# Seven-product (Strassen) form for 28 gate weight tiles ahead of the attention stage of a decoder layer

## What is computed

```python
mod = silu(c) @ w_ada + b_ada; shift, scale, gate = split(mod, 3)
h = rmsnorm(x, norm_w) * (1 + scale) + shift
aq, ak, av, az, mq, mk, mv, mo, mz, mi, mf, ga, gm = split(h @ w_in)
att = sliding_window_attention(rope(aq), rope(ak), av, sinks)       # 16 heads, 4 kv heads, window 128
y_att = (att * silu(az)) @ w_att
mq = silu(causal_conv(mq)); mk = silu(causal_conv(mk)) * 256 ** -0.5 # width 4
hm = mlstm(mq, mk, mv, mi, mf)                                       # 4 heads of 256
hm = rmsnorm(hm) * m_norm_w * sigmoid(mo)
y_m = (hm * silu(mz)) @ w_m
merged = sigmoid(ga) * y_att + sigmoid(gm) * y_m
out = rmsnorm(x + gate * (merged @ w_out), final_norm_w)
```

## Time and profile before

| | |
|---|---|
| median of 3 runs | 1346.77 us (1346.77, 1346.91, 1345.74) |
| span of the profiled execution | 1343.5 us |
| TensorE busy | 97% of the span |
| TensorE weight loads | 83% |
| VectorE | 48% |
| ScalarE | 32% |
| GpSimd | 45% |
| DMA over the span | 67 GB/s of mean |

### The profile page before, as it was taken

One profiled execution on the slowest core, in us unless ns is written; L12 is line 12 of the kernel. 1 busy time (PEld: TensorE's weight loads), 2 busy tenths in 40 slices (PEclk: granted clock), 3 DMA queues, 4 the chain that ended last, 5 costly groups with the idle time before them and its releaser, 6 DMA issues.

```text
span 1343.5 us, 20127 instructions
## 1 busy us (share of the span) xinstructions
PE 1308.8 (97%) x6941; PEld 1112.3 (83%) x6941; DVE 644.1 (48%) x1343; ACT 427.4 (32%) x1065; POOL 609.3 (45%) x824
## 2 busy tenths in 40 slices
PE   4899999999999999999999999999999999999997
PEld 3687988889788888889888988898889888788886
DVE  5776775857750000354554355435544421544335
ACT  5556564554630000133313332323232211311111
POOL 3507052160634444592665176517660555567240
PEclk9899999999999999999999999999999999999999
DMA  9702011020211310420410041004100133331602
GB/s 327 194 17 64 17 48 33 1 63 0 56 49 54 94 48 30 126 64 1 110 47 16 0 109 47 16 0 119 53 16 16 47 110 94 110 94 47 204 26 100
DMA packets 124951, 89.44 MB, mean 67 GB/s; under 512 B 12370, under 2 KB 117986, under 8 KB 124899
## 3 DMA queue, kind: packets, MB, share of 16 engines
q1 hardware_dynamic: 121056, 76.09, 20.2%
q10 hardware_dynamic: 3842, 12.68, 2.8%
HBM read 80.36 MB, written 8.41 MB: 66 GB/s over the span
## 4 chain that ended last, share of the span: by engine, by line
PE 92%; DVE 4%; ACT 2%; issue 1%; DMA 1%; ACTq 0%; POOL 0%; DVEq 0%
PE pp L574 27%; PE pp L575 26%; PE pp L576 26%; PE pp L742 2%; PE pp L853 2%; PE pp L725 1%; PE pp L726 1%; PE pp L733 1%; PE pp L662 1%; PE pp L845 1%; PE pp L710 1%; DVE prob_t L1485 1%; PE pp L648 1%; DMA freq<-inv_freq 1%; DVE pp L1423 1%
## 5 line engine op out<-in xcount | busy, mean ns | idle before, releaser
L513 POOL TENSOR_TENSOR w_hi<-raw,ones 128x256 fp32r<-128x256 f32 x388 | 263.9, 710 | 614.0 <-ACTq L371 342.3
L574 PE MATMUL pp<-h_hi,w_hi 128*128 128x512 f32 x896 | 349.9, 391 | 0.1
L575 PE MATMUL pp<-h_lo,w_hi 128*128 128x512 f32 x896 | 349.0, 390 | 0.0
L576 PE MATMUL pp<-h_hi,w_lo 128*128 128x512 f32 x896 | 348.8, 389 | 0.0
L517 POOL TENSOR_TENSOR w_lo<-raw,w_hi 128x256 fp32r<-128x256 f32 x388 | 319.7, 854 | 7.6
L576 PEld LDWEIGHTS pp<-h_hi,w_lo 128*128 128x128 f32 x896 | 168.2, 188 | 35.3
L574 PEld LDWEIGHTS pp<-h_hi,w_hi 128*128 128x128 f32 x896 | 168.3, 188 | 34.7 <-issue 0.7
L575 PEld LDWEIGHTS pp<-h_lo,w_hi 128*128 128x128 f32 x896 | 168.3, 188 | 33.5
L574 PE MATMUL pp<-w_hi,h_hi 128*128 128x256 f32 (+2 forms) x496 | 154.8, 312 | 2.0 <-ACT v_tok L1049 1.2
L576 PE MATMUL pp<-w_hi,h_lo 128*128 128x256 f32 (+2 forms) x496 | 153.1, 309 | 0.0
L575 PE MATMUL pp<-w_lo,h_hi 128*128 128x256 f32 (+2 forms) x496 | 152.9, 308 | 0.0
(11 more groups left out here) (259 smaller groups left out, 1928.1 us busy)
## 6 DMA issues: line engine op xcount, KB each, us to landing
raw<-w_in SPq DMA_DIRECT2D x70, 512.0 KB, 3.9
w_mod<-w_ada SPq DMA_DIRECT2D x6, 1024.0 KB, 12.7
x_in<-x SPq DMA_DIRECT2D x4, 1024.0 KB, 10.0
raw<-w_att SPq DMA_DIRECT2D x8, 512.0 KB, 5.6
merged_dram<-mix_a ACTq DMA_DIRECT2D x8, 512.0 KB, 2.6
w_gate<-w_ada ACTq DMA_DIRECT2D x8, 512.0 KB, 3.6
raw<-w_m SPq DMA_DIRECT2D x8, 512.0 KB, 3.8
mix_in<-merged_dram ACTq DMA_DIRECT2D x8, 512.0 KB, 3.3
```

The source lines that it names most:

```text
L513: ins = pool.tensor_tensor(hi[:, q, :], raw[:, s, q, :], one[:, q, :], ALU.mult)
L574: pe.matmul(o, lh, rh, start=first, stop=False)
L575: pe.matmul(o, lh, rl, start=False, stop=False)
L576: return pe.matmul(o, ll, rh, start=False, stop=last)
```

## The change

28 of the 32 tiles that only feed a sigmoid or a silu leave their stages: ga 2 to 7, gm 0 to 5, mz 0 to 7 and mo 0 to 7. They are computed in a new stage between the start and A, two tiles at a time, as 14 pairs (`GATE_PAIRS`: ga, gm and then mz with mo of the same number).

**Products.** For a pair the two weight tiles A and B and h are seen as 2 x 2 blocks (features in by two tiles; features in by two token halves), and the four blocks of the result come from 7 products by Strassen's scheme (Winograd's form) in place of 8. One product is 4 slices x 3 passes = 12 matmuls of 128x512 (`product`), into one of 8 banks; a later product of the same pair may accumulate onto a bank of an earlier one. The operand of a product is a block of weights or one of four differences and sums of blocks, `sums` and in place in `raw` (DVE `sum_of`, for the first two pairs partly GpSimd `first_sum`); ACT makes its high half (`operand_high`), GpSimd its low half (`operand_low`), in a ring of ten (`RING`). On the other side four combinations of h's quadrants are needed once, `t_hi` and `t_lo` (DVE `token_sum`, `token_low`; ACT `token_high`). DVE adds the products' banks into blocks (`add_first`, `add_seventh`, `block_22`, `block_21`, `block_12`), ACT applies sigmoid or silu (`gate_out`), and for mz with mo DVE multiplies the two and the norm weight (`gate_products`). SP stores the results to `sig_dram` and `gate_dram` and loads them again in B (`load_sig`), C (`gate_m`, one load a head) and D2 (`sig_m`).

**Start.** The loads of the first two pairs (four tiles of 512 KB) stand in SP's queue ahead of `load_mod(2)` and `load_mod(3)`. Product 0 stands ahead of the last `turn_mod`. `first_two_units` is gone: all eight token units of the first head are separate ones. The products of the first two pairs are interleaved.

**The stages that lost tiles.** B has 10 tiles (`B_TILES`). C has 16 units a head: mq, mk, mv, with the last chunk of a head behind mq 0 of the next and its transpositions behind mq 3; the mLSTM loop is unrolled, and its slots are 2, 3, 4, 2 for mq and mk and 0, 1 for mv. D1 has two tiles, gm 6 and 7, in slots 0 and 1, and holds the end of the last head between its units. `D_SLOTS` is now 2, 4, 0, 1. The gate sum is made in D2, one step behind each of eight units. E is as it was.

```diff
-SLOT_USES = {"A": (4,) * 5, "B": (4, 4, 4, 4, 0), "C": (8,) * 5,
-             "D1": (2, 2, 2, 0, 2), "D2": (2, 2, 2, 0, 2), "E": (1, 1, 1, 1, 0), "E2": (1, 1, 1, 1, 0)}
-SLOT_DMAS = {"A": (4, 3, 8, 4, 4), "B": (4, 4, 4, 4, 0), "C": (8,) * 5,
-             "D1": (2, 2, 2, 0, 2), "D2": (2, 2, 2, 0, 2), "E": (1, 1, 1, 1, 0), "E2": (1, 1, 1, 1, 0)}
-D_SLOTS = (0, 1, 2, 4)
+SLOT_USES = {"A": (4,) * 5, "B": (3, 3, 2, 2, 0), "C": (4, 4, 8, 4, 4),
+             "D1": (1, 1, 0, 0, 0), "D2": (2, 2, 2, 0, 2), "E": (1, 1, 1, 1, 0), "E2": (1, 1, 1, 1, 0)}
+SLOT_DMAS = {"A": (4, 3, 8, 4, 4), "B": (3, 3, 2, 2, 0), "C": (4, 4, 8, 4, 4),
+             "D1": (1, 1, 0, 0, 0), "D2": (2, 2, 2, 0, 2), "E": (1, 1, 1, 1, 0), "E2": (1, 1, 1, 1, 0)}
+D1_SLOTS = (0, 1)
+D_SLOTS = (2, 4, 0, 1)
 FIRST = 4
-BANK_USES = {"A": 24, "B": 16, "C": 48, "D1": 8, "D2": 8, "E": 8}
+GATE_SUM_AT = 3
+BANK_USES = {"A": 24, "B": 10, "C": 32, "D1": 2, "D2": 8, "E": 8}
 
...
-C_UNITS = [("mq", 0), ("mq", 1), ("mq", 2), ("mq", 3), ("mk", 0), ("mk", 1), ("mk", 2), ("mk", 3)]
-for _u in range(NB):
-    if _u % 2 == 0:
-        C_UNITS.append(("mz", _u // 2))
-    C_UNITS.append(("mv", _u))
-C_UNITS += [("mo", 0), ("mo", 1), ("mo", 2), ("mo", 3)]
-
-C_LOADS = [(MQ, 0, 0), (MQ + P, 1, 0), (MK, 2, 0), (MK + P, 3, 0), (MZ, 4, 0),
-           (MVC, 0, 1), (MVC + P, 1, 1), (MZ + P, 2, 1), (MO, 3, 1), (MO + P, 4, 1)]
+C_UNITS = [("mq", n) for n in range(4)] + [("mk", n) for n in range(4)] + [("mv", n) for n in range(NB)]
+
+C_LOADS = [(MQ, 2, 0), (MQ + P, 3, 0), (MK, 4, 0), (MVC, 0, 0), (MVC + P, 1, 0), (MK + P, 2, 1)]
+C_PER = {0: 1, 1: 1, 2: 2, 3: 1, 4: 1}
+
+B_TILES = [("ga", 0, 0, 0), ("wa", 0, 1, 0), ("ga", 1, 2, 0), ("wa", 1, 3, 0), ("wa", 2, 0, 1), ("wa", 3, 1, 1),
+           ("wa", 4, 2, 1), ("wa", 5, 3, 1), ("wa", 6, 0, 2), ("wa", 7, 1, 2)]
...
-C_SLOT = {"mq0": (0, 0), "mq1": (1, 0), "mk0": (2, 0), "mk1": (3, 0), "mz0": (4, 0), "mz1": (2, 1),
-          "mo0": (3, 1), "mo1": (4, 1)}
-C_MASK_AFTER = 2
+C_SLOT = {"mq0": (2, 0), "mq1": (3, 0), "mk0": (4, 0), "mk1": (2, 1)}
...
+GATE_PAIRS = [("a", 2), ("a", 4), ("a", 6), ("m", 0), ("m", 2), ("m", 4)] + [("o", t) for t in range(KT)]
...
+PRODUCTS = (1, 6, 7, 5, 2, 4, 3)
+EARLY = [(p, prod) for prod in (1, 5, 2, 3, 7, 6, 4) for p in range(2)]
+G_ORDER = EARLY + [(p, prod) for p in range(2, NG) for prod in PRODUCTS]
+G_AT = {pair_product: g for g, pair_product in enumerate(G_ORDER)}
+RING = 10
+FIRST_OPS = 4
+RING_OFF = (RING - 1 - (len(G_ORDER) - 1)) % RING
...
+TOKENS = {1: ("h", 0, 0), 2: ("h", 1, 0), 3: ("h", 1, 1), 4: ("t", 1, 0), 5: ("t", 0, 0), 6: ("t", 1, 1), 7: ("t", 0, 1)}
...
             load_mod(1)
+            for k in range(2):
+                for p in range(2):
+                    load_pair_slot(p, k)
             load_mod(2)
             load_mod(3)
...
+            def product(g):
+                p, prod = G_ORDER[g]
+                q, slot = p % 2, (g + RING_OFF) % RING
+                kind, kh, th = TOKENS[prod]
+                hi, lo = (h_hi, h_lo) if kind == "h" else (t_hi, t_lo)
+                o = bank({1: 0, 2: 0, 6: 2, 3: 4, 5: 4, 4: 6, 7: 6}[prod] + q)
...
+                t = slice(th * HALF, (th + 1) * HALF)
+                for k in range(HK):
+                    kt = kh * HK + k
+                    if p == 0 and kind == "h":
+                        pe.wait_ge(h_lo_ready, kt + 1)
+                    pe.matmul(o, op_hi[:, slot, k, :], hi[:, kt, t], start=first and k == 0, stop=False, skip_group_check=True)
+                    pe.matmul(o, op_hi[:, slot, k, :], lo[:, kt, t], start=False, stop=False, skip_group_check=True)
+                    ins = pe.matmul(o, op_lo[:, slot, k, :], hi[:, kt, t], start=False, stop=k == HK - 1, skip_group_check=True)
+                ins.then_inc(product_made, 1)
...
+            product(0)
             turn_mod(PAIRS - 1)
-            first_two_units()
-
+            for g in range(1, len(G_ORDER)):
+                product(g)
+            for s in range(3):
+                after(pe, slot_split[s], use("A", s, 1))
...
                     if kind == "mv" and n >= 1:
                         chunk(i, n - 1)
+                    if i and (kind, n) == ("mq", 0):
+                        chunk(i - 1, NB - 1)
+                    if i and (kind, n) == ("mq", 3):
+                        turn_heads(i - 1)
...
+            for k, s in enumerate(D1_SLOTS):
+                after(pe, slot_split[s], use("D1", s, 1))
+                for half in range(2):
+                    feature_unit("D1", 0, 0, 2 * k + half, s, half, h_hi, h_lo)
+                    if (k, half) == (0, 0):
+                        chunk(MH - 1, NB - 1)
+                    if (k, half) == (1, 0):
+                        turn_heads(MH - 1)
...
+            for k in range(2):
+                for half in range(2):
+                    b = full("D1", 0, 0, 2 * k + half)
+                    if half:
+                        free(act, D1_SLOTS[k])
+                    act.activation(sig_m[:, 6 + k, half * HALF:(half + 1) * HALF], bank(b), ACT.Sigmoid).then_inc(bank_free[b], 1)
+                    if (k, half) == (0, 0):
+                        head_end(MH - 1)
 
             after(act, ym_ready, 4 * MH)
             for k in range(FIRST):
-                act.activation(y2_first[k][:, :], y[:, k, 0:HALF], ACT.Copy).then_inc(y2_hi_ready, 1)
...
+            for p in range(2, NG):
+                last = p == NG - 1
+                if not last:
+                    sum_of(1, p + 1)
+                    sum_of(2, p + 1)
+                add_first(p)
+                gate_products(p - 1)
+                if not last:
+                    sum_of(3, p + 1)
+                add_seventh(p)
+                block_22(p)
+                block_21(p)
+                if not last:
+                    sum_of(4, p + 1)
+                block_12(p)
 
 
             for s, raw_s in ((1, raw_q[:, :, 1, :]), (2, raw[:, 2, :, :])):
                 after(dve, slot_hi[s], use("A", s, 1))
                 c = slice(s * P, (s + 1) * P)
                 dve.tensor_tensor(w0_lo[:, :, c], raw_s, w0_hi[:, :, c].bitcast(F32), ALU.subtract).then_inc(slot_split[s], 1)
+            gate_products(NG - 1)
+            for q in range(2):
+                dve.wait_ge(spilled[q], 16 * spills_before(NG + q))
...
+            def head_norm(i):
+                numerator(i, NB - 1)
...
+                        if i and (kind, n) == ("mq", 1):
+                            head_norm(i - 1)
...
+                        if GATE_SUM_AT <= n < GATE_SUM_AT + KT:
+                            sum_gate(n - GATE_SUM_AT)
...
```

861 lines of the change are left out of this document (574 added, 287 removed).

## The result

The changed kernel takes 1366.03 us (median of 4 runs, 1365.58 to 1370.10) against 1346.26 us before (1345.64 to 1346.91): the ratio is 1.0154, interval 1.0139 to 1.0168. It is slower by 19.8 us although TensorE has 168 matmuls less. Its profiled span is 1364.3 us, 20.8 us over the 1343.5 of before; 1364.6 us was forecast for the median.

The account below looks back on a forecast made before the run. TensorE, busy for 97% of the span, was taken as the bound: -38.1 + 2.5 + 3.9 + 27.2 + 2 + 4.7 + 3.4 + 12.2 = +17.8 us, a span of 1361.3 and median of 1364.6 us; range 1348 to 1378.

Parts of the forecast that it names:

- The work and its pace: New product stage: 168 fewer TensorE matmuls at an unchanged pace of 226.7 ns, -38.1 us.
- The rival by which a product waits for its operand all through the stage: New stage not bound by TensorE: 0.5 us lost in each of 84 products, +40; likelier 1372 to 1385; chance 0.13.
- The first transposition: Each head's first mk_t transposition loses mz's cover and waits 5.1 us; with restart 4 x 6.8, +27.2 us (19.2 without).
- The half speed behind it: TensorE's clock restarting at half speed after a wait of 3 us or more: 1.7 us each (0 to 1.8).
- Head boundaries: Between mLSTM heads: normalisation now precedes the next head's first convolution, freeing bank 0 late; three heads, +2 us (0 to 4).
- The "faster" rival: The mk_t wait is absent or under 1.5 us per head; at zero 1337.4 us; chance 0.12.
- E: E's first unit waits 10.5 us for GpSimd's splits of slots 1 and 2, plus restart: +12.2 us (9.5 to 13.5).
- my line on the gate sum: Gate sums moved into D2: one more DVE operation beside three of 0.69 us in a 5.44 us unit, costing nothing.
- D1: Before D1: slot 0, still used by mv 7, is split late; 3.1 us and a restart, +4.7 us (2.5 to 6).
- D2: D2's first unit: y_first copies behind D1's sigmoids, 2.3 us, then DVE's 0.85 us per slice; +3.4 us (2 to 5).
- the step to attention: First token unit waits 3.4 us for DVE's low halves behind the last block addition, plus restart: +3.9 us (1.5 to 6).
- The start: Up to the first products: quarter 2 later behind pair loads, then row copy and token sums; +2.5 us (-2 to +6).

Follow-up runs that it names:

- k_slots: Changed kernel with D1's tiles in slots 2 and 4 and D2's in 0, 1, 2, 4: 1360.50 us, ratio 1.0101.
- k_start: Changed kernel with ScalarE making the high halves of operands 6 and 7 ahead of the second token sum's high half: 1367.94 us, ratio 1.0156.
- k_loads: Changed kernel with the first two pairs' loads behind modulation quarter 2 in the DMA queue instead of ahead of it: 1368.72 us, ratio 1.0165.
- k_quiet: k_start with VectorE's low halves of the token sums for products 6 and 4 cut to 16 of 512 columns: 1364.48 us, ratio 1.0135.
- k_half: Changed kernel with the last key tile's convolution cut in two token halves, the first run beside mk 3: 1347.58 us, ratio 1.0008.
- k_mv1: Changed kernel with token units mv 0 and mv 1 both ahead of each head's first mk_t transposition: 1370.63 us, ratio 1.0173.
- k_all2: Changed kernel with split convolution, new slots, earlier gate sum, reordered joints, k_start's order and VectorE's token low halves waiting for GpSimd's tenth operand: 1319.55 us, ratio 0.9803.

## Why the prediction was right, and where it was not

**The work and its pace** held to a tenth: -38.1 us. The rival by which a product waits for its operand all through the stage fell: behind the ninth product none did.

**The first transposition** held in place, size and cause. 5.1 us were forecast and 5.0 measured in three heads, 3.8 in the last; the kernel before with its cover moved away shows the cause by itself. The half speed behind it was undersized, 2.15 us a head against 1.7, since I took the price from a stretch of another stage. Head boundaries: beside the wait and the half speed 1.2 us a head are lost, against 0.7. The "faster" rival, a wait under 1.5 us, is dead.

Within this term the size was partly luck. The working charged the wait in full, although a hole of 0.6 us per head went with it (2.4 us too much), took 5.1 us for the last head, which waits 3.8, and had half speed and boundaries too low; 29.2 forecast and 28.4 measured are sums of errors that cancel. (Its 19.2 for the case without any restart should read 4 x 5.1 = 20.4.) And one sentence of it is wrong: the convolution does shrink when GpSimd is quiet. The earlier trace rows could not show that: its shortest step took 1.52 us, and in the changed kernel steps go down to 1.28. There the first head's steps stand beside a split, the last head's do not:

```profile
805.84 1.12 DVE L2047 TENSOR_SCALAR conv<-xpad,vecs 128x1024 f32<-128x1024 f32 x1 [6.16 <-ACT xpad L1444]
807.00 4.73 DVE L2050 SCALAR_TENSOR_TENSOR conv<-xpad,vecs,conv 128x1024 f32<-128x1024 f32 x3
...
1092.44 0.75 DVE L2047 TENSOR_SCALAR conv<-xpad,vecs 128x1024 f32<-128x1024 f32 x1 [6.17 <-ACT xpad L1444]
1093.23 3.92 DVE L2050 SCALAR_TENSOR_TENSOR conv<-xpad,vecs,conv 128x1024 f32<-128x1024 f32 x3
```

```profile
805.23 3.76 POOL L647 TENSOR_TENSOR w_hi<-raw,ones 128x256 fp32r<-128x256 f32 x4 [24.14 <-ACTq L429]
...
1135.75 2.38 POOL L647 TENSOR_TENSOR w_hi<-raw,ones 128x256 fp32r<-128x256 f32 x4 [70.33 <-ACTq L429]
```

The four steps take 5.9 us beside a split and 4.7 without, which is the 1.2 us between the waits of 5.0 and 3.8; in k_slots, where GpSimd splits beside the last head's steps too, they take 5.8 and that wait is 4.9. So 1.2 us in each of the other three heads lie in the place of GpSimd's split, which no run here moved away.

**E** held: 10.5 us of wait forecast and 9.7 measured, 12.2 and 11.7 with the clock. GpSimd's last split ends at 1267.5, and TensorE starts at 1267.71:

```profile
1262.30 2.33 POOL L647 TENSOR_TENSOR w_hi<-raw,ones 128x256 fp32r<-128x256 f32 x4
1264.70 2.77 POOL L651 TENSOR_TENSOR w_lo<-raw,w_hi 128x256 fp32r<-128x256 f32 x4
```

But my line on the gate sum, "nothing", was only true as long as the slot order was worse. It is a DVE operation of no cost and a gate for four loads, and I had priced only the first; k_slots found it with 3.9 us.

**D1, D2 and the step to attention.** The waits, 2.8, 2.2 and 3.3 us, are those of the forecast (3.1, 2.3, 3.4), but in the profiled run none is followed by half speed, which was 1.7 too much for two of them. In D2 I also carried over DVE's pace of 0.85 us per slice from the earlier trace rows; the row of after has 0.60. GpSimd, which was busy for 6.0 of the 10.2 us beside it before, stands still for all but 0.6 of the 7.3:

```profile
1170.94 7.25 DVE L2085 TENSOR_TENSOR y_lo<-y,y_hi 128x512 fp32r<-128x512 f32 x12
```

And the wait for v_tok, which I said would go with two units ending together, is still there with 1.13 us.

**The start is the step that failed**: +2.5 with bounds -2 and +6, measured +11.3. The transposition of the last row came at 53.45 (52.6 forecast), with 1.7 us of half speed behind it, which puts the first six products 2.0 us behind the kernel before; by the working it would have been about 0.8 (an effective 50.3 against 50.6, and 1.1 of half speed). Then I let the seventh product wait 1.7 us. From start to start it came 5.8 us late, lost 1.6 in half speed, and the eighth and ninth came 1.2 and 0.7 late: 9.2 us. The working counted ScalarE's and VectorE's queue and took GpSimd's low halves as hidden. The first five of this row of the changed kernel take 2.2 to 2.8 us each beside VectorE's token sums, outside the 0.72 to 1.73 us of the earlier trace rows that I had quoted myself and then applied to the steady stage only:

```profile
69.72 15.19 POOL L670 TENSOR_TENSOR op_lo<-raw,op_hi 128x256 fp32r<-128x256 f32 x8 [6.43 <-ACT op_hi L1198]
```

The first two of these eight are the seventh product's; they end at 74.6, and the product starts at 74.72. At 0.73 us each they would end at 71.2, so by an estimate from these rows 3.4 of its 5.6 us of wait are this contention. Of the causes, k_start removes the queue and gains nothing, k_loads removes part of the transfer and loses, k_quiet removes the contention behind 78 us and gains 3.5 us. What the rest of the start is made of is read from the trace (the row copy behind the first token sum, the operations on VectorE in one row up to 82 us, the half-speed stretches) and was not tried apart.

So the sum came out 3.0 us low in span and 1.4 us low in the median: an error of 8.8 us in the start stood against one of 5.8 us the other way in the rest. The median came nearer than the span by luck as well: I put it 3.3 us above the profiled span, but in every run for which both are known the time is 1.7 to 1.8 us above its own span; the execution profiled before was one of the faster ones, not the median. The range held because its upper end had room for that, not because each term was right.

## What to carry to other kernels

Taking work off the busiest engine gives its full price only while something else still covers each latency; before a block is moved away, ask what chain was running beneath it, and start that chain earlier (k_half) rather than shuffle units in front of it (k_mv1). When an order of slots or a queue is mended, look at what the same tiles' loads wait for, since a second gate may stand right behind the first. With these few repairs the same change that lost 20 us wins 27.

## What the runs showed of the hardware

**GpSimd beside VectorE.** A GpSimd low half of 128x256 took 0.71 us with VectorE idle or in short operations, and 2.07 us on average, 2.8 at most, beside VectorE's long row of two-input operations on on-chip memory (k_start's rows). The Trainium skill (SBUF — State Buffer, SBUF: two separate sides) says that the two exclude each other in that case; the trace agrees, as five low halves in a row took as long as one VectorE operation each (2.8 us). It goes the other way too: four convolution steps of VectorE took 5.9 us beside a split and 4.7 without. k_quiet and k_all2 show that it is worth 3.5 us where GpSimd is waited for. A wait put on VectorE made the kernel faster.

**The clock behind short waits is not fixed by the wait.** The granted clock of the rows tells it, and the first matmul alone does not: half speed can begin some matmuls later, as behind D1's wait of 2.8 us in k_quiet (columns as in the windows above):

```profile
1137.60:1139.20 1.60, 1.57 (x7) 1.31 (x8) 0.00 (x0) 1.43 (x3) 1.60 (x3) 0.99 0.00 0
1139.30:1142.60 3.30, 3.30 (x9) 2.52 (x9) 0.00 (x0) 0.00 (x0) 3.22 (x5) 0.50 0.00 0
```

Behind the first 40 us, waits of 3.8 us or more at one stretch were followed by half speed in all profiles here, at once or within 1.3 us. Shorter ones, which the prediction thought might pass, went both ways: the 3.3 us before the first token unit were followed by it in eight profiles of nine, the 2.8 us before D1 in six of eight, the 2.2 us before D2 in five of nine. The changed kernel and k_start have none behind D1 and D2, k_quiet and k_loads have it behind both, with the same waits ahead of them in the heads; so the waits in the heads alone do not decide it. What does was not tried. The same kernel can so be 7 us apart from run to run, as k_half was.
